# Small steps of the first recurrence enter TensorE's order only when the planner's clock says that their PSUM banks are free

## The reference, cut to what matters

```
qkv = silu(causal_dwconv(qkv, conv_w)); q, k = l2norm(q), l2norm(k)
a_mat = where(strict, einsum('bhncd,bhnsd->bhncs', kb, k) * gamma, 0)
t_mat = triangular_solve(eye + a_mat, eye)            # one inverse for each chunk
u, w  = t_mat @ (v * beta), t_mat @ (kb * exp(gc))
state, o = scan(step, 0, ...)                          # step: v_new = u - w @ state; ...
y_a = (rms_norm(o) * silu(z)) @ w_branch_a
merged = sigmoid(gate_a) * y_a + sigmoid(gate_b) * y_b
x = x + merged @ w_out
```

## Time and profile before

| | us |
|---|---|
| median of 3 runs | 2870.69 |
| lowest and highest | 2870.43, 2870.78 |
| the profiled execution | 2873.41 |
| its span, first to last instruction | 2871.6 |
| its mean granted PE clock | 0.988 |

### The profile page before, as it was taken

One profiled execution on the slowest core, in us unless ns is written; L12 is line 12 of the kernel. 1 busy time (PEld: TensorE's weight loads), 2 busy tenths in 40 slices (PEclk: granted clock), 3 DMA queues, 4 the chain that ended last, 5 costly groups with the idle time before them and its releaser, 6 DMA issues.

```text
span 2871.6 us, 39894 instructions
## 1 busy us (share of the span) xinstructions
PE 2791.0 (97%) x15956; PEld 2426.7 (85%) x15956; DVE 1876.8 (65%) x2230; ACT 1503.2 (52%) x2042; POOL 148.6 (5%) x123
## 2 busy tenths in 40 slices
PE   7999999999999999999999998999999999999998
PEld 5899887888888888888888997877888888888886
DVE  5457765545568777777777676766666666666665
ACT  5456545444455454555456566545554444444464
POOL 0000111000000000000000022111000000000000
PEclk9999999999999999999999999999999999999999
DMA  6554533465665666656665532222565666566654
GB/s 212 183 172 148 162 118 110 143 194 185 189 198 185 192 194 190 189 187 190 192 191 176 188 111 74 90 73 94 178 189 192 188 194 192 186 196 189 193 170 161
DMA packets 133817, 485.23 MB, mean 169 GB/s; under 512 B 15072, under 2 KB 16352, under 8 KB 133120
## 3 DMA queue, kind: packets, MB, share of 16 engines
q1 hardware_dynamic: 133632, 482.68, 53.5%
HBM read 480.53 MB, written 2.10 MB: 168 GB/s over the span
## 4 chain that ended last, share of the span: by engine, by line
PE 85%; DVE 7%; ACT 4%; issue 3%; DMA 1%; POOL 0%; DVEq 0%; ACTq 0%; SPq 0%; POOLq 0%
PE psm L185 78%; PE psb L185 6%; ACT ar L201 2%; DVE ar L223 1%; PE psb L188 1%; DVE ar L213 1%; DMA raw<-in_w_in 1%; DVE slo L213 1%; ACT shi L201 1%; DVE x L213 1%; DVE gs L223 0%; DVE ar L227 0%; ACT L201 0%; ACT hf L201 0%; DVE gf L213 0%
## 5 line engine op out<-in xcount | busy, mean ns | idle before, releaser
L213 DVE TENSOR_TENSOR slo<-raw,shi 128x1024 fp32r<-128x1024 f32 (+1 forms) x901 | 1112.8, 1240 | 641.9 <-ACT shi L201 639.1
L201 ACT ACTIVATE shi<-raw 128x1024 fp32r<-128x1024 f32 (+1 forms) x901 | 946.1, 1053 | 998.5 <-PE psm L185 803.7
L185 PE MATMUL psm<-shi,gs 128*128 128x512 f32 x2272 | 727.8, 395 | 9.7 <-DVE slo L213 8.8
L185 PE MATMUL psm<-hs,shi 128*128 128x512 f32 (+1 forms) x2528 | 565.1, 347 | 0.0
L185 PEld LDWEIGHTS psm<-shi,gs 128*128 128x128 f32 x2272 | 429.7, 189 | 100.0 <-DVE slo L213 9.2
L185 PEld LDWEIGHTS psm<-hs,shi 128*128 128x128 f32 x2528 | 428.4, 190 | 47.6 <-issue 0.6
L185 PE MATMUL psm<-gs,shi 128*128 128x512 f32 (+2 forms) x2080 | 456.9, 341 | 2.4 <-DVE slo L213 2.4
L185 PE MATMUL psm<-shi,hs 128*128 128x512 f32 x1408 | 450.1, 393 | 4.0 <-DVE hs L213 2.9
L185 PE MATMUL psm<-slo,gs 128*128 128x512 f32 x1136 | 444.9, 392 | 0.0
L185 PEld LDWEIGHTS psm<-gs,shi 128*128 128x128 f32 (+1 forms) x2080 | 351.9, 191 | 40.1 <-DVE slo L213 3.0
L185 PE MATMUL psm<-hs,slo 128*128 128x256 f32 x1968 | 355.7, 283 | 0.0
(11 more groups left out here) (184 smaller groups left out, 1644.6 us busy)
## 6 DMA issues: line engine op xcount, KB each, us to landing
raw<-in_w_in SPq DMA_DIRECT2D x240, 512.0 KB, 3.9
raw<-in_w_up SPq DMA_DIRECT2D x176, 512.0 KB, 3.7
raw<-in_w_ffn_up SPq DMA_DIRECT2D x128, 512.0 KB, 4.3
raw<-in_w_ffn_down SPq DMA_DIRECT2D x128, 512.0 KB, 4.3
raw<-in_w_down SPq DMA_DIRECT2D x88, 512.0 KB, 3.6
raw<-in_w_out SPq DMA_DIRECT2D x64, 512.0 KB, 4.0
raw<-in_w_ple_gate SPq DMA_DIRECT2D x32, 512.0 KB, 4.3
raw<-in_w_branch_b SPq DMA_DIRECT2D x16, 512.0 KB, 3.7
```

Of the source, the lines that this page charges most:

```text
L185: return self.issued(self.eng and self.eng.matmul(out, lhs, rhs, start=start, stop=stop, skip_group_check=True), cost)
L201: return self.issued(self.eng and self.eng.activation(out, in_, fn, scale=scale, **kw), cost)
L213: return self.issued(self.eng and self.eng.tensor_tensor(out, a, b, op), self.cost(out))
```

## The change

A new object `Free(banks, n)` stands for "n banks are free", and its `time()` is the n-th earliest planned end among the readers of the banks' present contents; a bank whose reader is not placed yet does not count, and a bank never used counts as 0. Every step of `gdn` and of its inverses that takes banks now lists it among its wanted events, with n the number of banks that it takes. The step then becomes due at the later of two times: its data plus the slack of 1.5, and the planned end of the n-th bank's reader plus `HOP` (0.1), with no slack. The second recurrence (`pair`) runs the same `inverse` but gets no such condition (`tag[0] == "gdn"`). The slack moves from `ready` into `due`, so the lane that goes first among several is now chosen by data plus slack or bank.

```diff
+    def free(self, n):
+        return Free(self, n)
+class Free:
+    def __init__(self, banks, n):
+        self.banks, self.n = banks, n
+    def time(self):
+        b = self.banks
+        times = sorted(0.0 if u is None else b.given[u][0].time(b.given[u][1]) for u in b.now if u is None or u in b.given)
+        return times[self.n - 1] if len(times) >= self.n else 0.0
...
-                    yield [(dve_step, (tag, "Y", n)), (act_step, (tag, "R", n))]
+                    yield [(dve_step, (tag, "Y", n)), (act_step, (tag, "R", n))] + ([banks.free(1)] if tag[0] == "gdn" else [])
...
-                    yield [(dve_step, (tag, "X", n + 1))]
+                    yield [(dve_step, (tag, "X", n + 1))] + ([banks.free(2 if n < 5 else 1)] if tag[0] == "gdn" else [])
...
-                    yield [(act_step, ("gT", hp))]
+                    yield [(act_step, ("gT", hp)), banks.free(2)]
...
-                    yield []
+                    yield [banks.free(1)]
                     b = four(banks.take(pe, ("qk", hp)))
...
                     yield [(pool_step, ("mt0", hp)), (pe_step, ("qk", hp))]
-                    yield []
+                    yield [banks.free(2)]
                     b = four(banks.take(pe, ("vn", hp)))
...
             def known(w):
+                if isinstance(w, Free):
+                    return True
                 return w() if callable(w) else w[1] in w[0].at
             def due(w):
-                return max([c[0].time(c[1]) + HOP for c in want[w] if not callable(c)], default=0.0)
+                data = max([c[0].time(c[1]) + HOP for c in want[w] if not callable(c) and not isinstance(c, Free)], default=-99.0)
+                return max([data + slack[0]] + [c.time() + HOP for c in want[w] if isinstance(c, Free)])
...
-                while ws := [w for w in open_lanes() if due(w) + slack[0] <= max(pe.t, until)]:
+                while ws := [w for w in open_lanes() if due(w) <= max(pe.t, until)]:
```

More of the change, by code:

```diff
@@ L892, in inverse @@
                 trs([(m4[:, m // 2, m % 2, :], mt[:, m, :]) for m in range(4)], (tag, "mt"))
-                yield [(dve_step, (tag, "X", 0)), (pool_step, (tag, "eye"))]
+                yield [(dve_step, (tag, "X", 0)), (pool_step, (tag, "eye"))] + ([banks.free(2)] if tag[0] == "gdn" else [])
                 pe.wait_ge(pool_step, (tag, "eye"))
@@ L913, in inverse @@
                 trs([(b[:, 128 * m:128 * m + 128], inv.S[:, 0, m, :]) for m in range(2)], (tag, "last"))
-                yield [(act_step, (tag, "last"))]
+                yield [(act_step, (tag, "last"))] + ([banks.free(1)] if tag[0] == "gdn" else [])
             def gdn(w):
@@ L946, in gdn @@
                     trs([(b[:, 128 * i:128 * i + 128], gk[:, h, 0:128]) for i, h in enumerate(hs)], ("kd", hp))
-                    yield [(dve_step, ("mt", hp))]
+                    yield [(dve_step, ("mt", hp)), banks.free(1)]
                     yield from inverse(("gdn", hp), inv, mt, (dve_step, ("mt", hp)))
@@ L953, in gdn @@
                         ("u0", hp))
-                    yield [(act_step, ("u0", hp))]
+                    yield [(act_step, ("u0", hp)), banks.free(1)]
                     pe.wait_ge(act_step, ("u0", hp))
@@ L957, in gdn @@
                     mms([(b[:, 128 * i:128 * i + 128], kd[:, i, :], u0[:, i, :], i == 0, True) for i in range(2)], ("S", hp))
-                    yield [(act_step, ("S", hp)), (pool_step, ("kg", hp))]
+                    yield [(act_step, ("S", hp)), (pool_step, ("kg", hp)), banks.free(1)]
                     pe.wait_ge(act_step, ("S", hp))
@@ L963, in gdn @@
                          for i, h in enumerate(hs)], ("v1", hp))
-                    yield [(dve_step, ("v1", hp))]
+                    yield [(dve_step, ("v1", hp)), banks.free(1)]
                     pe.wait_ge(dve_step, ("v1", hp))
@@ L968, in gdn @@
                         ("u1", hp))
-                    yield [(act_step, ("u1", hp)), (dve_step, ("qkt", hp))]
+                    yield [(act_step, ("u1", hp)), (dve_step, ("qkt", hp)), banks.free(1)]
                     pe.wait_ge(act_step, ("u1", hp))
@@ L978, in gdn @@
                     mms(lst, ("go", hp))
-                    yield [(act_step, ("gsq", hp))]
+                    yield [(act_step, ("gsq", hp)), banks.free(1)]
                     pe.wait_ge(act_step, ("gsq", hp))
@@ L984, in gdn @@
                     yield [(act_step, ("groot", hp))]
-                    yield [(dve_step, ("grec", hp)), (dve_step, ("z", 0)), (dve_step, ("z", 1))]
+                    yield [(dve_step, ("grec", hp)), (dve_step, ("z", 0)), (dve_step, ("z", 1)), banks.free(2)]
                     pe.wait_ge(dve_step, ("grec", hp))
```

## The result

The changed kernel takes 2856.47 us (median of 4 runs, 2856.09 to 2860.02) against 2870.74 for the kernel before. The ratio is 0.9950, 95% interval 0.9936 to 0.9964: 14.3 us faster. The profiled execution took 2856.33 us, its span 2854.5, with a mean clock of 0.991.

What follows compares the result with a forecast made beforehand. The prediction took PE, busy 97% of the span, as the bound, with waits for banks in the recurrence. 12.4 us won less 1.2 staying gave 11.2, so 2870.69 became 2859.5 us, range 2856.8 to 2866.

Steps and rivals of the forecast that it cites:

- the two holes: PE's idle stretches in the recurrence, 3.2 and 4.1 us, before lane 1's `kk` and `qk`, waiting for banks.
- Step A and B of lane 1 at the first place: Near 364 us, weights fill the waits before `kk` and `qk`: 5.10 us won, plus 0.90 from the clock.
- The sum: Gain from weights filling both holes at full clock, idle time and clock losses together: 12.4 us.
- The second place: Near 465 us, head pairs 2 and 3, weights fill the same waits: 4.76 us, plus 1.61 from the clock.
- The other conditions: Step C, the inverses, `u0` to `gb`: banks are free there, delays cost nothing, up to 0.8 us may be won.
- What stays: Waits left before lane 1's `qk` because DVE is later than planned: 0.6 us per place, 1.2 in all.
- The cover and the weights: Weight work hides later small steps up to `branch_a`, and buffered weights suffice: 5.7 us against 5.1, 5.4 against 4.8.
- rival (d): Weights run out: PE waits for late `slo` in the recurrence, two such waits give 2877.1 us; chance 0.06.
- (a): Step B of lane 1 waits as now, 2.25 us, and the clock falls: gain 7.1, 2863.6 us; chance 0.15.
- (b): Short waits left over still halve the clock, only removed waits count: 5.2 us won, 2865.5; chance 0.08.
- (c): The wait only moves, same four banks, `kk` waits later: gain 0 to 3, 2867.7 to 2870.7 us; chance 0.08.

Runs made afterwards that it cites:

- the rest alone: The changed kernel without the bank conditions of steps A and B, all other conditions kept: 2863.62 us, ratio 0.9970 to the kernel before.
- A and B for the first pairs only: The kernel before with the bank conditions of steps A and B for head pairs 0 and 1 only: 2864.78 us, ratio 0.9975.
- filled holes: The kernel before with extra matmuls of constants, read by nothing, where PE waits before lane 1's `kk` and `qk`: 2869.66 us, ratio 0.9993.
- another start: The kernel before, no bank condition, both lanes' start put off in the plan until the second half of `z` leaves PSUM: 2861.53 us, ratio 0.9968.
- step A alone: The kernel before with only the condition of two free banks before `gc` and `kk`: 2867.91 us, ratio 0.9984.
- A and B alone: The kernel before with only two free banks asked for step A and one for step B: 2865.83 us, ratio 0.9981.
- one event: The kernel before, no bank condition, lane 1's step A also waiting in the plan for lane 0's `mt`: 2860.76 us, ratio 0.9961.

## Why the prediction was right and where it was wrong

**What bounds the kernel, and the two holes.** Right. PE's idle time and the clock behind it were the whole matter. Behind 678 us the two profiled executions differ by another 1.7 us, less than the 2.7 by which the one before lay above its median, so no change there is shown.

**Step A and B of lane 1 at the first place.** Right, by the timeline above. With all else left out, the edits win 5.5 us there and in what follows; with all else present (the change against the rest alone, 0.9950 against 0.9970, intervals that just overlap) they add 5.7, by the stage time 6.4. The sum said 5.10 + 0.90 for this place.

**The second place.** A step that failed: "goes behind its own `gT`" and the picture of weights between two lanes' steps, 4.76 + 1.61 us of the sum. There `kk` and `qk` stand together (471.49). The gain was found, but by another way, and it doesn't hang on steps A and B: the rest alone brings it too. In the kernel before, these rows of DVE and PE stand ahead of it:

```profile
451.45 1.22 DVE L223 SCALAR_TENSOR_TENSOR ar<-ar,psm 128x1024 f32<-128x1024 f32 x1 [2.48 <-PE psm L185]
452.77 1.75 DVE L227 RECIPROCAL ar<-ar 64x256 f32<-64x256 f32 x1
...
459.78 0.70 PE L185 MATMUL psb<-hf,con 32*128 32x256 f32 x4
462.59 1.05 PE L185 MATMUL psb<-con,ar 128*128 128x128 f32 x8
```

and these, at the same point of the work, in the kernel after:

```profile
440.10 1.22 DVE L223 SCALAR_TENSOR_TENSOR ar<-ar,psm 128x1024 f32<-128x1024 f32 x1 [0.93 <-PE psm L185]
...
447.56 1.75 DVE L227 RECIPROCAL ar<-ar 64x256 f32<-64x256 f32 x1 [0.56 <-ACT ar L201]
```

Line 223 takes the first `branch_b` group out of PSUM. Before, it stood in DVE's order in front of lane 0's reciprocal and waited 2.48 us for PE to finish the group; lane 0 came out late, and both lanes began their second pair together. After, PE is further in the weights, the group's end falls earlier, and the reciprocal waits for ACT alone. That DVE row can be a part of the meeting, but not all of it: with all the rest alone it stands in front of the reciprocal (at 450.96) again, and the lanes come apart all the same:

```profile
448.67 1.22 DVE L223 SCALAR_TENSOR_TENSOR ar<-ar,psm 128x1024 f32<-128x1024 f32 x1 [1.60 <-PE psm L185]
```

And in the change lane 0's `gc` comes 4.4 us earlier but lane 1's 5.3 us later, which that row doesn't account for. That it is a meeting, and no property of the steps there, is shown by four runs without conditions on A and B at that place in which lane 1's `gc` comes 10 us or more after lane 0's by itself (all the rest, A and B for the first pairs only, filled holes, another start). Which of the shifts moved the lanes in the changed kernel was not separated, and the cause of the meeting stays open.

**The other conditions, costed at nothing, up to 0.8 us won.** Wrong, and this is the step that puts the time below the range: the term was put at nothing. Alone they win 8.6 us (8.2 by the stage time), and without them A and B win 5.5 (6.6) where the sum had 11.2: once the lanes are apart, the inverses of lane 0 meet the first steps of lane 1, and the wait for a bank turns up there (2.8 us and a lower clock). I had argued from a trace in which the lanes stood together, where those steps had banks; the change itself moved the lanes. The view had it, too: in the earlier trace rows idle time is 3.19 + 4.14 = 7.3 us, and the clock at 0.91 costs 0.09 x 40 = 3.6 twice, 14.5 together by estimate, against 14.3 won and 0.17 left. The short waits behind the holes and the clock until full speed are in that sum and weren't in mine.

**What stays, 1.2 us.** Too much. PE waits 0.17 us at one place. The planner's `gT` is 0.34 us too short, but it is made up for along the way, and 0.5 us more on each bank's time changes nothing that shows. With the residue at 0.2 instead of 1.2, the sum would be 12.2 and the forecast 2858.5; the rest of the miss is the term above.

**The cover and the weights.** Right. PE has no wait from the last small step to the first transposes at 678.38, and none for `slo` in the stage, so rival (d) had no part in it. The recurrence ended 3 us later in time (562.55 for 559.58) with 18 us more of weights done.

**The rivals.** (a) is what step A alone shows: `qk` waits 1.36 us at the first place, without a fall of the clock there. (b) didn't come, because a single wait of 0.17 us was left, with the clock at 1.00. Its mechanism isn't ruled out: with step A alone one wait of 1.20 us was followed by a granted clock of 0.62 (shown below). (c) is half true: four banks were enough once the lanes were apart, but with A and B alone the wait did move, to `gb` and to `Y`. The Trainium skill says that a repeated gap can mean too little PSUM (Perfetto Trace Analysis, section Optimization Strategy); here the gaps went without another bank.

## What to carry to other kernels

A planned order that ignores a resource makes the strictly ordered engine wait for it where two users meet; putting the resource's free time among a step's conditions won 14.3 us here, where the engine had other work and the chain had time to spare, and 2.8 us, within the intervals, in the second recurrence. When a change moves one of two interleaved chains, price every later meeting anew, and take the idle time and clock of the whole stage as the upper bound, not the holes that stand out. Before writing a rule, try a different start or an offset between the chains: here one event or a later start gave about two thirds of the gain or more.

## What the runs showed of the hardware that was not expected

The length of a single wait of PE doesn't say whether the clock falls. Waits of 2.4 to 2.8 us were followed by half clock in three of the runs (weight matmuls 0.43 us apart instead of 0.227), and one of 1.36 us at the first place and two of 1.25 and 1.45 us with another start were not (granted 1.00 over 361 to 378, 390 to 455 and 500 to 508). In the kernel before, the eight instructions behind a wait of 1.91 us still took 1.16 us, while those behind 2.24 us took 2.08. And with step A alone a wait of 1.20 us for `gb`, at 463.56, was, and with A and B alone one of the same length, at 460.76, wasn't. Of the windows of PE, first with step A alone:

```profile
464.00:468.50 4.50, 4.50 (x14) 3.41 (x13) 3.67 (x4) 1.77 (x5) 3.96 (x3) 0.62 0.00 0
```

and then with A and B alone:

```profile
455.00:464.00 9.00, 7.79 (x45) 6.30 (x44) 6.20 (x10) 4.79 (x7) 2.42 (x2) 1.00 0.35 117
```

The granted clock stands third from the end: 0.62 behind the one wait, 1.00 around the other. What tells the two apart stays open. Matmuls of constants in place of the idle time at the first place kept the clock at 1.00 (12.88 of 13.2 us busy).
